# The input product of a hybrid block in fp32r high and low parts, with a reordered modulation and a reordered front

## The chip, the cores and the metric

The kernel runs on 1 core of one Trainium2 chip. The metric is the device time of one execution in microseconds. It is written by hand for the five engines (TensorE, VectorE, ScalarE, GpSimd and the DMA queue of SyncE); each engine runs its own list of instructions in order, and semaphores tie them together.

## The reference, cut to what matters

The sequence has 512 tokens (T), the model 1024 columns (D). One layer is computed:

```python
cond = silu(c)
mod = cond @ w_ada + b_ada                      # 6 x 1024: shift1, scale1, gate1, shift2, scale2, gate2
n1 = rms_norm(h, g_norm1) * (1 + scale1) + shift1
z  = n1 @ w_in                                  # 1024 -> 3840: conv GLU input | q | k | v | gate logits
branch_a = conformer_conv(z[:, :1024])          # GLU, depthwise conv over 31 taps, layer norm, swish, 512 -> 1024
attn = window_attention(q, k, v, sinks)         # 8 heads, own chunk and the one before
branch_b = attn @ w_attn_out
merged = sigmoid(gA) * branch_a + sigmoid(gB) * branch_b
h = h + gate1 * (merged @ w_out)
n2 = rms_norm(h, g_norm2) * (1 + scale2) + shift2
h = h + gate2 * peer(n2)                        # product-key retrieval over 16384 experts
out = rms_norm(h, g_final)
```

The change touches everything up to `n2`. The PEER part behind it is the same in both kernels.

## The kernel before

All activations lie transposed, columns of the model on the 128 partitions and the 512 tokens along them: `hT` and `nT` are 8 such tiles (KT = 8) of 128x512. A tile of the input product is 128 output columns by 512 tokens: 8 matmuls that accumulate over k into one PSUM bank. The product has 30 such tiles: 8 for the convolution (a GLU half and its gate in turn), 4 for q, 1 for k, 1 for v (which is computed the other way round, tokens on the partitions, in 4 x 8 matmuls of 128x128), and 16 for the gates.

**Modulation.** `w_ada` comes as 48 chunks of 128x1024 (0.5 MB), 8 for each of the six rows of `mod`, through a ring of four in `low` (`load_ada`, L293). VectorE multiplies each chunk by one column of `cond` and adds it up in `macc` (L1032, L1035). TensorE then sums `macc` over the partitions with 8 matmuls against a single column of ones (`modulation`, L495). The first 16 chunks are needed for `n1`; the others are taken in between the convolution's GLU products, and their sums over the partitions stand inside the attention, in `att_scores` at a = 3, 5, 7 and 9.

**Head.** SyncE issues four chunks, then `xT`, then the other twelve. ScalarE squares `hT`, TensorE sums the squares (`column_sums`, L488), VectorE makes the reciprocal of the root, scales `hT` into `nT`, and ScalarE applies scale and shift (`modulate`, L788).

**Input product.** `product` (L503) is a plain fp32 matmul; in the profile one fp32 matmul appears as two MATMUL records. Weights come as pairs of tiles (1 MB) through the ring of four pairs `wring`; the q, k and v weights have a place of their own (`qkvw`, 3 MB in one load). Convolution tiles and q, k, v run through four PSUM banks in turn (`bank`, `bank_free`).

**Attention.** 16 steps `att_out(a)`, a = 4 b + m for four token blocks b and four pairs of heads m. TensorE's order within a step is: transposes of the probabilities (L570, waits for `p_ready`), scores of step a+2 (L548), gate tile a+1 (L503), output product (L582, waits for `pt_ready`). VectorE adds the bias, takes the maximum, and divides by the sum (`att_norm`, L1078), and works off the convolution's taps in between: 124 taps (31 for each of four tiles) of one `scalar_tensor_tensor` over 128x512 (L1092), 44 of them ahead of the attention. ScalarE takes the exponentials (L832), copies the transposed probabilities out (L818), once per block the output (L821, waits for `o_done`), and the gate tiles (L825).

**Behind it.** Sum for the layer norm, attention projection and convolution projection (fp32, L503), merged with the gates by VectorE; then the output product `w_out`, which already works in two parts: ScalarE rounds a weight tile to fp32r (`wout_round`, L855), VectorE takes the remainder (`wout_rest`, L1155), and TensorE forms high x high, high x low and low x high in 24 matmuls for a tile (L640). Then the second norm and the PEER part: query product, selection of keys on VectorE and GpSimd, and dense expert products in fp32r (L702, L744) to the end.

Of the kernel before, what the change touches and what calls it, by code (L numbers as in the profile page):

```python
# [7 lines left out]
P = 128  # L8
D = 1024
T = 512  # L10
KT = D // P
TB = T // P
CT = 4
TAPS = 31
TAPS_BEFORE = 11
# [32 lines left out]
R_CONV, R_GATE, R_PROJ, R_WOUT, R_PQ, ROUNDS = 0, 1, 3, 4, 5, 7  # L48
MODS = 6

# [11 lines left out]
N_WOUT = N_PROJ + 2 * KT - 4  # L62
# [6 lines left out]
def build(nc, stream, wada, wqkv, skT, xT, cols, rows, biasd, identd, puT, pu, pv, gmat, hsave, out):  # L69
# [4 lines left out]
    with ExitStack() as ctx:  # L74
# [10 lines left out]
        place.close()  # L85
        big = sb("big", [P, 22 * D])
# [5 lines left out]
        qkvw = mid[:, :].rearrange("p (j k c) -> p j k c", j=6, k=KT)  # L92
# [18 lines left out]
        wparts = place.enter_context(nc.sbuf_tensor("wparts", [P, 2, 2, D], f32r))  # L111
        place.close()
        ptsb = sb("ptsb", [P, 2, 4, P])
# [39 lines left out]
        macc = gates[:, 2 * KT - 2 * MODS:2 * KT, :].rearrange("p (q a) t -> p q (a t)", q=MODS)  # L153
# [58 lines left out]
        MOD2 = ps[:, 3, KEYS:KEYS + MODS * KT]  # L212

# [3 lines left out]
        qkvw_here = sem("qkvw_here")  # L217
# [5 lines left out]
        ada_used, macc_ready = sem("ada_used"), sem("macc_ready")  # L223
# [55 lines left out]
        def _(sp):  # L279
            sp.dma_start(colv[:, :], cols).then_inc(small_here, 16)  # L280

            def load_round(r, wait):
                for s in range(4):
                    if wait:
                        sp.wait_ge(pair_begun, r * 4 + s - 2)
                    sp.dma_start(wring[:, s, :, :, :].rearrange("p a b c -> p (a b c)"),
                                 stream[bass.ds(r * 4 + s, 1), :, :].rearrange("a p f -> (a p) f")
                                 ).then_inc(w_here[s], 16)
            def load_ada(g, wait):
                for e in range(4):  # L290
                    if wait:
                        sp.wait_ge(ada_used, g * 4 + e - 3)
                    sp.dma_start(aring[:, e, :], wada[bass.ds(g * 4 + e, 1), :, :].rearrange("a p f -> (a p) f")  # L293
                                 ).then_inc(ada_here[e], 16)
            load_ada(0, False)
            sp.dma_start(hT, xT).then_inc(x_here, 16)
            with sp.Fori(1, 2 * KT // 4) as g:
                load_ada(g, True)
            load_round(0, False)
            sp.dma_start(mid[:, :], wqkv).then_inc(qkvw_here, 16)  # L300
            with sp.Fori(2 * KT // 4, MODS * KT // 4) as g:
                load_ada(g, True)
            sp.dma_start(ident[:, :], identd).then_inc(late_here, 16)
            sp.dma_start(rowv[:, :], rows).then_inc(late_here, 16)
            sp.wait_ge(ada_used, MODS * KT)
            sp.dma_start(bias, biasd).then_inc(late_here, 16)
            sp.dma_start(skw, skT).then_inc(late_here, 16)
            with sp.Fori(1, ROUNDS) as r:
                load_round(r, True)
# [7 lines left out]
            sp.wait_ge(pair_begun, 4 * (ROUNDS - 1) + 2)  # L317
# [60 lines left out]
        def _(pool):  # L378
            nc.gpsimd.memset(ones[:, :], 1.0).then_inc(consts, 1)
            nc.gpsimd.memset(eps[:, :], EPS).then_inc(consts, 1)  # L380
# [10 lines left out]
            nc.gpsimd.memset(zeros[:, :], 0.0).then_inc(consts, 1)  # L391

# [84 lines left out]
        def _(pe):  # L477
# [5 lines left out]

            def column_sums(n, sq0, count):
                o = bank(n)
                for k in range(count):
                    pe.wait_ge(sq_ready, sq0 + k + 1)
                    mm = nc.tensor.matmul(o, ones[:, :], sq[:, (sq0 + k) % 2, :], start=(k == 0), stop=(k == count - 1))  # L488
                    mm.then_inc(sq_used if k < count - 1 else tile_done, 1)

            def modulation(q):

                pe.wait_ge(macc_ready, q + 1)
                for c in range(KT):
                    mm = nc.tensor.matmul((MOD if q < 2 else MOD2)[:, q * KT + c:q * KT + c + 1], macc[:, q, c * P:(c + 1) * P], ones[:, 0:1],  # L495
                                          start=True, stop=True)
                return mm
# [16 lines left out]
            for s in range(4):  # L514
                pe.wait_ge(w_here[s], (R_CONV + 1) * 16)
                for j in range(2):
                    mm = product(bank(N_CONV + 2 * s + j), lambda k: wring[:, s, j, k, :], lambda k: nT[:, k, :], begins=j == 0,
                                 need=0 if s == 0 and j == 0 else None)
                    mm.then_inc(tile_done, 1)


            pe.wait_ge(qkvw_here, 16)
            for j in range(5):
                mm = product(bank(N_QKV + j), lambda k: qkvw[:, j, k, :], lambda k: nT[:, k, :])
                mm.then_inc(tile_done, 1)
            o = bank(N_QKV + 5)
# [976 lines left out]
```

## Time and profile before

| | us |
|---|---|
| median of 3 runs | 1781.67 |
| lowest, highest | 1777.55, 1782.49 |
| the profiled execution's own time | 1778.79 |
| its span | 1776.4 |

The profiled execution's time is 2.4 us more than its span, and lies 2.9 us below the median. The page gives, for each engine, busy time and its share of the span. A stage's busy time says which engine leads there, and the chain of waits says what TensorE waited for. A granted clock of 1.00 stands for 2.4 GHz and one of 0.50 for 1.2 GHz.

| stage | from, to (us) | what runs |
|---|---|---|
| head | 0, 41.9 | first norm, modulation rows 0 and 1 |
| convolution tiles and q, k, v | 41.9, 141.1 | 14 tiles of the input product |
| attention | 141.1, 289.3 | 16 steps, 16 gate tiles |
| projections, output product | 289.3, 395.4 | |
| second norm, PEER | 395.4, 1776.4 | same in both kernels |

### The profile page before, as it was taken

What the parts mean: (1) busy time and instruction counts of PE and PEld (TensorE: products, weight loads), DVE (VectorE), ACT (ScalarE), POOL (GpSimd) and SP (SyncE); (2) the same over time, 40 slices, a digit from 0 to 9 for tenths busy, and PEclk for the clock granted to TensorE, in tenths of its full rate; (3) what the DMA queues carried; (4) which work ended last, traced back from release to release, by engine and by line L of the source; (5) the groups of instructions that cost most, each with busy time, mean ns of one, the idle gap of its engine ahead of it and who ended that gap; (6) DMA issues with size and microseconds to landing.
All of it is one profiled execution on the core that took longest, in us unless ns stands there. A gap on an engine that the chain in (4) does not pass through costs nothing. (4 is left out here: it accounts for less than half of the span.)

```text
span 1776.4 us, 23708 instructions
## 1 busy us (share of the span) xinstructions
PE 1679.0 (95%) x7829; PEld 1331.5 (75%) x7829; DVE 1352.0 (76%) x2820; ACT 543.3 (31%) x751; POOL 442.4 (25%) x386
## 2 busy tenths in 40 slices
PE   3999999998998799898999999999999999999995
PEld 2445544474446799897898998989889989898984
DVE  6677664534999799995878787878787877878787
ACT  2102233223112356663322223232222222323222
POOL 0000000001456500001333333333343343334330
PEclk8999999999998999999999999999999999999998
DMA  9951110321212235457897878888888888788872
GB/s 358 337 218 48 57 62 24 112 79 53 90 36 72 72 137 211 164 202 289 301 320 277 325 275 312 288 296 302 294 296 298 310 288 307 282 320 325 325 289 96
DMA packets 137982, 388.46 MB, mean 219 GB/s; under 512 B 9408, under 2 KB 58816, under 8 KB 132160
## 3 DMA queue, kind: packets, MB, share of 16 engines
q1 hardware_dynamic: 99904, 251.33, 39.7%
q0 software_dynamic: 36864, 134.23, 20.4%
q10 hardware_dynamic: 1152, 2.10, 0.3%
q8 instruction: 35, 0.57, 0.1%
q14 instruction: 27, 0.22, 0.0%
HBM read 358.26 MB, written 29.36 MB: 218 GB/s over the span
## 5 line engine op out<-in xcount | busy, mean ns | idle before, releaser
L702 PE MATMUL ps<-xs,Us 128*128 128x384 f32 x3072 | 566.4, 340 | 12.6 <-POOL Us L427 10.2
L702 PEld LDWEIGHTS ps<-xs,Us 128*128 128x128 f32 x3072 | 544.4, 190 | 23.2 <-POOL Us L427 12.1
L744 PE MATMUL ps<-Vs,As 128*128 128x512 f32 x2304 | 544.0, 392 | 5.9 <-DVE Vs L1373 5.9
L744 PEld LDWEIGHTS ps<-Vs,As 128*128 128x128 f32 x2304 | 432.5, 188 | 93.4 <-DVE Vs L1373 5.8
L503 PE MATMUL ps<-big 128*128 128x512 f32 (+1 forms) x784 | 327.7, 577 | 9.8 <-ACT big L788 9.8
L503 PEld LDWEIGHTS ps<-big 128*128 128x128 f32 x784 | 144.3, 193 | 179.4 <-issue 175.3
L975 ACT ACTIVATE att<-ps 128x384 f32<-128x384 f32 x96 | 47.2, 492 | 594.2 <-PE ps L702 594.2
L463 POOL DMA_INDIRECT big<-pv,islot x128 | 156.5, 1223 | 211.1 <-DVE low L1390 174.0
L463 POOL DMA_INDIRECT big<-pu,islot x128 | 144.3, 1128 | 218.0 <-DVE dot L1378 182.9
L1364 DVE TENSOR_TENSOR att<-att 128x384 f32<-128x384 f32 x96 | 53.4, 557 | 161.5 <-ACT att L975 151.6
L1390 DVE SCALAR_TENSOR_TENSOR low<-big,act_w,low 128x1024 f32<-128x1024 f32 x128 | 158.5, 1280 | 1.2 <-DMA big<-pv,islot 1.2
L1373 DVE TENSOR_TENSOR Vs<-big,Vs 128x1024 fp32r<-128x1024 f32 x128 | 156.0, 1219 | 3.1 <-ACT Vs L978 3.1
L978 ACT ACTIVATE Vs<-big 128x1024 fp32r<-128x1024 f32 x128 | 134.9, 1054 | 68.6 <-PE ps L744 56.7
L1378 DVE CUSTOM_DVE_ANT_0 big<-big,ptsb 128x1024 f32<-128x1024 f32 x128 | 151.4, 1221 | 0.0
L890 ACT ACTIVATE Us<-big 128x1024 fp32r<-128x1024 f32 x128 | 134.3, 1049 | 36.4 <-DMA big<-puT 35.1
L454 POOL COPY islot<-eidx 128x8 int32 (+1 forms) x32 | 31.8, 993 | 367.7 <-DMA gmat<-big 208.2
L1350 DVE TENSOR_TENSOR Us<-big,Us 128x1024 fp32r<-128x1024 f32 x95 | 116.0, 1221 | 4.3 <-ACT Us L890 2.1
L388 POOL TENSOR_TENSOR xs<-big,xs 128x384 fp32r<-128x384 f32 x8 | 7.8, 1009 | 412.9 <-ACT xs L874 412.9
L729 PE MATMUL ps<-low 128*128 128x128 f32 x768 | 93.2, 280 | 15.1 <-ACT big L948 8.6
L1339 DVE TENSOR_SCALAR low<-iotan,att 128x128 f32<-128x128 f32 x384 | 106.9, 344 | 0.0
L729 PEld LDWEIGHTS ps<-low 128*128 128x128 f32 x768 | 91.7, 196 | 16.3 <-DVE low L1339 10.0
L948 ACT ACTIVATE big<-ps 128x512 f32<-128x512 f32 x96 | 93.6, 1140 | 5.6 <-PE ps L729 5.6
(163 smaller groups left out, 1296.2 us busy)
## 6 DMA issues: line engine op xcount, KB each, us to landing
big<-puT SPq DMA_DIRECT2D x128, 512.0 KB, 4.9
big<-pv SPq DMA_DIRECT2D x64, 1024.0 KB, 8.9
big<-stream SPq DMA_DIRECT2D x28, 1024.0 KB, 4.8
low<-wada SPq DMA_DIRECT2D x48, 512.0 KB, 5.2
gmat<-big SPq DMA_DIRECT2D x12, 2048.0 KB, 7.3
att<-gmat SPq DMA_DIRECT2D x32, 768.0 KB, 9.5
big<-wqkv SPq DMA_DIRECT2D x1, 3072.0 KB, 19.9
big<-xT SPq DMA_DIRECT2D x1, 2048.0 KB, 11.2
```

Of the source, the lines that this page charges most:

```text
L463: nc.gpsimd.indirect_dma_start(out=row[:, r % ROWBUF, :], out_offset=None, in_=table, in_offset=bass.IndirectOffsetOnAxis(ap=islot[:, half ...
L503: mm = nc.tensor.matmul(o, lhs(k), rhs(k), start=(k == 0), stop=(k == count - 1))
L702: mm = nc.tensor.matmul(ps[:, 6 + e, 0:DT], a, xs[:, b, k, :], start=(k == 0 and a is hi and b == 0), stop=(k == KT - 1 and a is lo))
L729: mm = nc.tensor.matmul(ps[:, c, t * P:(t + 1) * P], ohj[:, 4 * c + t, :], ohi[:, 4 * c + t, :], start=True, stop=True)
L744: mm = nc.tensor.matmul(ps[:, 2 * b + half, :], a, Vs[:, e, w, half * T:(half + 1) * T], start=False, stop=(last and a is lo))
L890: f(Us[:, e, 0, :], uraw[:, e, :], ACT.Copy).then_inc(uhi_ready, 1)
L978: f(Vs[:, d % 2, 0, :], vraw[:, d // 2 % 2, d % 2, :], ACT.Copy).then_inc(vhi_ready, 1)
L1339: mm = v.tensor_scalar(ohi[:, 4 * c + t, :], iotan[:, :], lists[:, 0, tok:tok + 1], lists[:, 2, tok:tok + 1], ALU.is_equal, ALU.mult)
L1350: v.tensor_tensor(Us[:, e, 1, :], uraw[:, e, :], Us[:, e, 0, :].bitcast(f32), ALU.subtract).then_inc(ulo_ready, 1)
L1373: v.tensor_tensor(Vs[:, a, 1, :], vraw[:, d // 2 % 2, d % 2, :], Vs[:, a, 0, :].bitcast(f32), ALU.subtract).then_inc(vlo_ready, 1)
L1378: v.tensor_tensor_reduce(out=row[:, s % ROWBUF, :], in0=row[:, s % ROWBUF, :], in1=n_tok, scale=1.0, scalar=0.0, op0=ALU.mult, op1=ALU.add ...
L1390: v.scalar_tensor_tensor(acc[:, s % 2, :], row[:, s % ROWBUF, :], act_w[:, bass.ds(g * DOTS + (s - SLOTS), 1)], acc[:, s % 2, :], ALU.mult ...
```

## The change

**Input product in parts.** Each tile of it is now formed as `w_out` is: ScalarE rounds the weight tile to fp32r (`w_round`, into a ring of HIS = 3 high parts `whi`), another engine subtracts the rounded from the full weight (`wlo`), and TensorE runs `three`: high weight x high n1, high x low, low x high, 24 fp32r matmuls for a tile in place of 8 fp32 ones. The v tile does the same with 96 matmuls of 128x128. `n1` is split too: ScalarE writes the rounded `ahi` (`n1_round`), VectorE the full value (`n1_fp32`) and the remainder `alo` (`n1_rest`). The first two tiles advance together over k. VectorE makes the weight remainders of tiles 0 to 16 (`w_rest`); GpSimd makes those of the last 13 gate tiles, during the attention.

**Modulation.** Chunks 0 to 15 are no longer added up by VectorE: TensorE takes each in 8 fp32 matmuls with a single column of `cond` as the moving operand (`eat`), one chunk behind each of the 8 sums of squares and then 8 more. Chunks 16 to 23 go through VectorE among the convolution tiles, chunks 24 to 47 through VectorE behind the attention (their loads wait for the scores of the last step); row 2 is summed over the partitions at a = 3 of the attention, rows 3 to 5 between the output product and the second norm's sums.

**Loads.** `xT` now goes ahead of all chunks. The q, k, v weights come through the ring of pairs, as tiles 8 to 13.

**Attention.** Two gate tiles run ahead (AHEAD = 2), the division by the sum moves to ScalarE (`att_scale`, two instructions, behind the gate tile's copy and the rounding), the sink's exponential is two instructions, taps are spread as 5 in a step, 47 of them ahead of the attention.

**Projections.** All 8 attention projections run ahead of the 8 convolution projections, with the layer norm's sums in between.

```diff
-            pe.wait_ge(consts, 1)
-            column_sums(N_RMS1, 0, KT)
-            modulation(0)
-            modulation(1).then_inc(mod_done, 1)
+            def eat(i):
+                q, k = divmod(i, KT)
+                pe.wait_ge(ada_here[i % 4], 16 * (i // 4 + 1))
+                for c in range(KT):
+                    mm = nc.tensor.matmul(MOD[:, q * KT + c:q * KT + c + 1], ada_slot(i)[:, c * P:(c + 1) * P],
+                                          cond[:, k:k + 1], start=False,
+                                          stop=(i == 2 * KT - 1 and c == KT - 1))
+                mm.then_inc(ada_eaten, 1)
...
+            def three(o, j, k, begins=False):
+                hi, lo = whi[j % HIS][:, k * P:(k + 1) * P], wlo[:, j // 2 % 4, j % 2, k, :]
+                for w, a in ((hi, ahi), (hi, alo), (lo, ahi)):
+                    mm = nc.tensor.matmul(o, w, a[:, k, :], start=(k == 0 and w is hi and a is ahi),
+                                          stop=(k == KT - 1 and w is lo))
...
+            o = bank(N_RMS1)
+            for k in range(KT):
+                column_sum(o, 0, k, KT)
+                eat(k)
+            for k in range(KT):
+                eat(KT + k)
+            pe.wait_ge(wlo_ready, 2)
+            pair = [bank(N_CONV), bank(N_CONV + 1)]
+            for k in range(KT):
+                pe.wait_ge(n1lo_ready, k + 1)
+                for j in range(2):
+                    mm = three(pair[j], j, k, begins=(j == 0 and k == 0))
...
-                if a + 1 < TB * PAIRS:
-                    gate_tile(a + 1)
+                if a + AHEAD < TB * PAIRS:
+                    gate_tile(a + AHEAD)
...
+            pe.wait_ge(attn_merged, KT)
+            for q in range(3, MODS):
+                mm = modulation(q)
+            mm.then_inc(mod_done, 1)
             column_sums(N_RMS2, KT + CT, KT)
...
+            def w_round(j):
+                p = j // 2
+                act.wait_ge(w_here[p % 4], w_count(p))
+                if HIS <= j < 2 * P_GATE + HIS:
+                    act.wait_ge(tile_done, N_CONV + j - HIS + 1)
+                elif j >= HIS:
+                    act.wait_ge(gate_done, j - HIS - 2 * P_GATE + 1)
+                f(whi[j % HIS], wring[:, p % 4, j % 2, :, :].rearrange("p k c -> p (k c)"), ACT.Copy).then_inc(whi_ready, 1)
...
                 if a >= 1:
                     att_evac(a - 1)
-                    gate_evac(a - 1)
+                gate_evac(a)
+                if 2 * P_GATE + a + HIS < FRONT:
+                    w_round(2 * P_GATE + a + HIS)
+                att_scale(a)
...
+            for j in range(2 * P_GATE + HIS, FRONT):
+                pool.wait_ge(whi_ready, j + 1)
+                pool.wait_ge(wlo_ready, j)
+                nc.gpsimd.tensor_tensor(wlo[:, j // 2 % 4, j % 2, :, :].rearrange("p k c -> p (k c)"),
+                                        wring[:, j // 2 % 4, j % 2, :, :].rearrange("p k c -> p (k c)"),
+                                        whi[j % HIS].bitcast(f32), ALU.subtract).then_inc(wlo_ready, 1)
```

## Rows read from the trace of the kernel before

**Rows 1.** Page: the span, and TensorE's busy time, share and instructions.
```profile
span 1776.4 us, 23708 instructions
PE 1679.0 (95%) x7829; PEld 1331.5 (75%) x7829; DVE 1352.0 (76%) x2820; ACT 543.3 (31%) x751; POOL 442.4 (25%) x386
```

**Rows 2.** Busy time by stage: PE, PEld, DVE, ACT, POOL, clock, DMA share, GB/s.
```profile
0.00:41.90 41.90, 14.13 (x48) 8.48 (x49) 26.55 (x25) 9.32 (x14) 0.81 (x8) 0.84 0.92 353
41.90:141.10 99.20, 98.28 (x272) 47.40 (x273) 70.90 (x84) 12.31 (x19) 0.00 (x0) 0.98 0.70 260
141.10:289.30 148.20, 147.49 (x552) 71.78 (x552) 91.82 (x211) 36.07 (x115) 0.00 (x0) 0.99 0.16 57
289.30:395.40 106.10, 106.10 (x339) 63.40 (x338) 44.49 (x57) 32.59 (x36) 0.00 (x0) 1.00 0.22 80
```

**Rows 3.** DMA rate over the first 20 us, one value per 0.5 us.
```profile
GB/s 0 0 0 37 275 262 377 369 393 410 262 254 295 393 377 492 475 557 328 360 459 492 459 360 426 344 385 352 442 426 418 410 410 434 426 401 270 279 311 295
```

**Rows 4.** ScalarE in order of time: start, us, line, tiles, idle before.
```profile
14.34 1.15 ACT L778 ACTIVATE att<-big 128x512 f32<-128x512 f32 x2 [11.37 <-DMA big<-xT]
226.09 0.60 ACT L821 ACTIVATE attnT<-ps 128x512 f32<-128x512 f32 x1 [9.39 <-PE ps L582]
```

**Rows 5.** TensorE in order of time, the same columns.
```profile
23.83 1.84 PE L495 MATMUL ps<-ones,gates 128*128 128x1 f32 x16
34.60 3.58 PE L495 MATMUL ps<-ones,gates 128*128 128x1 f32 x16 [8.93 <-DVE gates L1035]
177.93 8.83 PE L503 MATMUL ps<-big 128*128 128x512 f32 x16
227.23 7.13 PE L503 MATMUL ps<-big 128*128 128x512 f32 x16
236.11 7.13 PE L503 MATMUL ps<-big 128*128 128x512 f32 x16
351.00 44.52 PE L640 MATMUL ps<-mparts,wparts 128*128 128x512 f32 x192
```

**Rows 6.** Short stretches with TensorE's granted clock, columns as in rows 2.
```profile
34.60:38.20 3.60, 3.58 (x16) 3.49 (x16) 3.40 (x2) 0.00 (x0) 0.00 (x0) 0.50 1.02 430
42.00:45.00 3.00, 3.00 (x4) 1.41 (x5) 1.34 (x3) 3.00 (x5) 0.00 (x0) 0.50 1.05 451
...
175.00:178.00 3.00, 3.00 (x27) 2.48 (x27) 0.00 (x0) 0.38 (x1) 0.00 (x0) 1.00 0.03 5
178.50:181.50 3.00, 3.00 (x5) 1.35 (x4) 2.83 (x10) 0.00 (x0) 0.00 (x0) 0.50 0.28 49
195.50:198.50 3.00, 3.00 (x30) 2.81 (x32) 0.00 (x0) 1.08 (x2) 0.00 (x0) 1.00 0.00 0
```

**Rows 7.** Matmul groups by shape: count, busy us, mean ns of one, idle before.
```profile
L702 PE MATMUL ps<-xs,Us 128*128 128x384 f32 x3072 | 566.4, 340 | 12.6 <-POOL Us L427 10.2 <-issue 2.1 <-DVE Us L1350 0.3
L503 PE MATMUL ps<-big 128*128 128x128 f32 x64 | 7.3, 275 | 0.0
```

**Rows 8.** Groups by shape on ScalarE, VectorE and GpSimd, columns as in rows 7.
```profile
L855 ACT ACTIVATE wparts<-big 128x1024 fp32r<-128x1024 f32 x8 | 8.4, 1057 | 31.5 <-PE ps L640 25.0 <-DMA big<-stream 6.4
L788 ACT ACTIVATE big<-big,mod,coef 128x512 f32<-128x512 f32 x16 | 11.5, 802 | 19.2 <-DVE coef L1047 14.9 <-DVE big L1017 4.3
...
L1373 DVE TENSOR_TENSOR Vs<-big,Vs 128x1024 fp32r<-128x1024 f32 x128 | 156.0, 1219 | 3.1 <-ACT Vs L978 3.1
L1092 DVE SCALAR_TENSOR_TENSOR work<-work,colv 128x512 f32<-128x512 f32 x120 | 80.9, 746 | 0.0
...
L427 POOL TENSOR_TENSOR Us<-big,Us 128x1024 fp32r<-128x1024 f32 x11 | 28.0, 2553 | 10.4 <-ACT Us L890 10.1 <-POOL attnT L412 0.3
```

**Rows 9.** One VectorE group twice, and GpSimd beside the second, by time.
```profile
442.30 0.69 DVE L1258 TENSOR_TENSOR big<-att 128x64 f32<-128x64 f32 x5
...
588.49 2.49 DVE L1258 TENSOR_TENSOR big<-att 128x64 f32<-128x64 f32 x5
...
586.98 2.37 POOL L407 TENSOR_TENSOR low<-low,att 128x1024 f32<-128x1024 f32 x1
```

More of the change, by code:

```diff
@@ L308, in _ @@
-            with sp.Fori(1, ROUNDS) as r:
-                load_round(r, True)
+            for p in range(4, P_WOUT):
+                load_pair(p)
+            sp.wait_ge(s_done, TB * PAIRS)
+            for i in range(3 * KT, 4 * KT + 4):
+                load_ada(i)
+            load_pair(P_WOUT)
+            for i in range(4 * KT + 4, 5 * KT):
+                load_ada(i)
+            load_pair(P_WOUT + 1)
+            for i in range(5 * KT, 5 * KT + 4):
+                load_ada(i)
+            load_pair(P_WOUT + 2)
@@ L311, in load_u @@
+            load_pair(P_WOUT + 3)
+            for i in range(5 * KT + 4, CHUNKS):
+                load_ada(i)
+            sp.wait_ge(ada_used, CHUNKS - 2 * KT)
+            sp.dma_start(skw, skT).then_inc(skw_here, 16)
+            for p in range(P_PQ, STREAM):
+                load_pair(p)
             def load_u(n, e):
@@ L522, in _ @@
[L522 to L524 removed]
+            def three(o, j, k, begins=False):
[3 more added lines that the diff above has]
+                                          stop=(k == KT - 1 and w is lo))
+                    if begins and w is hi and a is ahi:
+                        mm.then_inc(pair_begun, 1)
+                return mm
@@ L525, in _ @@
                 mm.then_inc(tile_done, 1)
-            o = bank(N_QKV + 5)
+            j = 2 * P_GATE - 1
+            o = bank(N_CONV + j)
+            pe.wait_ge(wlo_ready, j + 1)
             for b in range(TB):
-                mm = product(o[:, b * P:(b + 1) * P], lambda k: nT[:, k, b * P:(b + 1) * P], lambda k: qkvw[:, 5, k, :])
+                for k in range(KT):
+                    hi, lo = whi[j % HIS][:, k * P:(k + 1) * P], wlo[:, j // 2 % 4, j % 2, k, :]
+                    for a, w in ((ahi, hi), (alo, hi), (ahi, lo)):
+                        mm = nc.tensor.matmul(o[:, b * P:(b + 1) * P], a[:, k, b * P:(b + 1) * P], w,
+                                              start=(k == 0 and a is ahi and w is hi), stop=(k == KT - 1 and w is lo))
@@ L589, in _ @@
             att_scores(1)
-            gate_tile(0)
+            for g in range(AHEAD):
+                gate_tile(g)
             for a in range(TB * PAIRS):
@@ L1059, in _, with glu @@
+            def glu(m):
                 n = N_CONV + 2 * m
@@ L1145, in _ @@
                 v.tensor_tensor(y[:, m, :], y[:, m, :], rstd, ALU.mult).then_inc(yn_ready, 1)
+            chunk(3 * KT + 1)
+            for d in range(3, KT):
+                attn_merge(d)
+                chunk(3 * KT + d - 1)
+            chunk(4 * KT - 1)
             def merged_rest(d):
```

475 lines of the change are left out of this document (282 added, 193 removed).

## Prediction

> **What bounds the kernel now.** The page comes first: TensorE is busy for 95% of the span [rows 1], so time is won only where its own work gets shorter or a wait of its goes away. The split by stage says where: in the convolution, q, k, v stage, in the attention and in the projections TensorE is busy for 98.3 of 99.2, 147.5 of 148.2 and 106.1 of 106.1 us, while VectorE has 71 to 92 us of the first two and ScalarE 12 to 36 [rows 2]. There TensorE's matmul time is the stage's length, and the other engines have room. The head is another matter: TensorE is busy for 14 of 41.9 us, and the DMA queue moves 353 GB/s at 92% busy [rows 2]; the first 16 modulation chunks and x are 10.5 MB, and they set its end. The last thing to read is TensorE's clock: the head ran at 0.84 on average, and the short stretches show which work it did before the clock rose or fell [rows 6].
>
> **The tile in parts.** The 14 tiles took 98.28 us; less 7.3 for the v tile [rows 7] and 1.6 for the start at 1.2 GHz (half of the 3.1 us from 41.9 to 45.0) [rows 6], 13 fp32 tiles took 89.4, or 6.88 each. The output product has the new form already: 192 matmuls for 8 tiles in 44.52 us [rows 5], or 5.57 a tile, with rounding and remainders hidden. So a tile saves 1.31 us. The v tile goes from 64 records in 7.3 us to 96 matmuls of 128 columns, which no row shows in fp32r. Lower bound: at the old rate of a record, (7.3 / 64) x 96 = 11.0. Upper bound: at the pace of the 384-column fp32r matmuls, 566.4 / 3072 = 0.184 each, 17.7; at a whole fp32 matmul each (0.228) 21.9. It would be 5.9 at best, if time went by columns alone (0.184 / 3). I take 11.0, since weight loads are as many and as wide as in the old record. **Convolution, q, k, v: -13 x 1.31 + 3.7 = -13.3.**
>
> The side work there is hidden: for a tile a rounding of 1.05 us on ScalarE and a remainder of 1.22 on VectorE [rows 8] beside 5.57 of matmuls. VectorE also has up to 5 taps of 0.67 (80.9 / 120), together 4.6 us, and a GLU product in every second tile. A chunk of modulation takes about the time of a remainder, and 16 chunks have left VectorE. Were this cover gone, each tile would wait some tenths.
>
> **The head.** Now TensorE does 16 chunks of 8 single-column matmuls. The same form is in the trace twice: 8 of them took 1.84 us at full clock and 3.58 at half clock [rows 5, 6]. Adding up the rates of the first 20 us [rows 3], x and the small columns (2.2 MB) are there at 8.2 us, where ScalarE waited for x until 14.3 before [rows 4]; the first sum starts at 9.0. A sum of squares is 0.86 (an eighth of 6.88), 1.72 at 1.2 GHz. A chunk comes each 1.5 us (0.5 MB at 353 GB/s) and is then no longer what is waited for: TensorE needs 1.84 or 3.58.
> Which clock? At 34.6 TensorE ran single-column matmuls for 3.58 us without a pause and the clock stayed at 0.50 to their end and beyond; full-width matmuls from 41.9 on brought it to 2.4 GHz after 45 (the convolution stage as a whole has 0.98) [rows 2, 6]. At 175 it was never idle, did transposes, the single-column matmuls and scores for 3 us, and the clock fell to 0.50 all the same; the full-width tile behind took 8.83 instead of 7.13 [rows 5, 6]. The same mixture at 195.5 kept 1.00 [rows 6]. I read: single-column matmuls do not lift the clock, and may lose it. In the new head they take two thirds of TensorE's time up to the eighth sum, and all of it behind that. I take 1.2 GHz throughout: 9.0 + 8 x (1.72 + 3.58) + 8 x 3.58 = 80.0. Then coefficients 0.4, two `n1_round` of 0.72 (11.5 / 16), two roundings of 1.05, a remainder of 1.22 [rows 8]: the first product starts at 85.2, against 41.9. **Head: +43.3.** At full clock it would be 9.0 + 8 x 2.70 + 8 x 1.84 + 1.7 (start at half clock) = 47.0, and 52.2 with the rest: +10.3. This is the term that decides.
> By the Trainium skill (TensorE: Matmul & The Clock Gate, the section on the HAM clock gate) the halved clock is the default and activity releases it; single-column matmuls aren't set apart. By that alone the head would come out at the +10.3; the row at 34.6 speaks against it here.
>
> **Attention.** A step lasts 8.88 us, from gate tile to gate tile [rows 5]. 16 gate tiles save 16 x 1.31 = 21.0. Three of four modulation sums leave (3 x 1.84 = 5.5), and the tile of 8.83 loses 1.7. Against that stands a new wait. `att_scale` is on ScalarE's queue. At a = 4, 8 and 12 ScalarE waits for the block's last output product, as it did before at 226.09 [rows 4], but now behind that wait are queued the output's copy (0.6), a gate copy (0.6), `w_round` (1.05) and the two scalings (0.4 each, estimated as half of 0.72 for half the width), and TensorE's next transposes wait for the last. TensorE has nothing to do meanwhile, since the gate tile stands behind the transposes: 3.0 each, 9.0. The second last step has no gate tile any more to cover ScalarE: 1.0. The pauses follow on small matmuls, so I add the price of a half-clock stretch, 1.7, at 0.7 of three places: 3.6. Between the ends of 0 and 5.1. **-21.0 - 5.5 - 1.7 + 9.0 + 1.0 + 3.6 = -14.6.**
>
> GpSimd's 13 remainders take 2.55 us each [rows 8], and were idle time there; one is wanted each 7 us or more, two steps ahead. They can slow VectorE: five small adds took 0.69 alone and 2.49 while a GpSimd operation of 2.37 ran [rows 9]. At worst 13 x 2.55 = 33 us come on top of VectorE's 92, 125 in all against some 133 of stage: hidden as a sum, and I take 0. The Trainium skill (SBUF — State Buffer, Who interferes with whom) says a VectorE instruction with two SBUF inputs contends with a GpSimd one that reads SBUF, and whoever comes second is fully blocked; the trace agrees [rows 9]. Every tap is of that kind, so this speaks against giving the remainders to GpSimd, where VectorE itself would need 1.22.
>
> **Behind it.** fp32 projections are the same in number, 106.1 us with TensorE never idle [rows 2]. The first now waits for ScalarE's last copy: 0.9. VectorE has a chunk more per tile, and two remainders at d = 5, so the last `merged_rest` comes about 1.5 late. Three modulation sums come between output product and second norm, where nothing covers them: 5.5. They are single-column again, so part of them and of the sums of squares behind runs at 1.2 GHz: 3.0 (from 0 to 5.5). **+10.9.** The q, k, v weights in the ring, later loads (SyncE now waits for the last scores before chunk 24) and `skT` come when DMA is at 16 to 22% [rows 2]: 0. PEER is unchanged: 0.
>
> **Sum.** +43.3 - 13.3 - 14.6 + 10.9 = +26.3. On the profiled execution's 1778.8 that gives 1805.1. That execution lies 2.9 below the median, well inside the range.
>
> **Rivals.**
> 1. Head at full clock (the page's rule): 33.0 less, -6.7, 1772.1: faster. For it: 195.5 kept its clock, and each sum of squares is a full-width matmul. Against it: 34.6 and 175 [rows 6]. It decides from the clock being above half for nearly all of the 16 chunks; break-even is a head of about 59 us. 0.10.
> 2. The first eight chunks, mixed with sums, at full clock, the last eight at half: 9.0 + 21.6 + 1.7 + 28.6 = 60.9, 19.1 less, +7.2: 1786.0, about no change. 0.14.
> 3. Half clock, and in addition GpSimd's lock makes VectorE late in each step (13 x 0.5 = 7), or the v tile costs its upper 17.7 to 21.9 (7 to 11 more): 1812 to 1823. 0.10.
> 4. The parts do not pay in the front (weights come late, a tile still takes 6.88): 29 x 1.31 = 38 more, 1843. The output product's rows speak against it. 0.02.
> My forecast has 0.64.
>
> **How the numbers follow.** The forecast's own range is 1789 (v tile 5.9, no half-clock patches, shorter waits) to 1816. About 0.3% is what a measurement of this kernel can tell from no change. Faster: rival 1 and a little error of the sum in rival 2, 0.14. Same: most of rival 2, 0.11. Slower: the forecast, rivals 3 and 4 and a rest of 2, 0.75. The range 1781 to 1821 leaves out rival 1 and the ends.
>
> **What would show it.** The granted clock and the length of the single-column matmuls between 9 and 80 us: pieces of 3.58, then the first full-width tile at 85; pieces of 1.84 and a start at 52 would refute me. Tiles of 5.5 us between; v tile near 11; three idle times of 3 us of TensorE released by ScalarE's scaling; three modulation sums ahead of the second norm. If the product starts at 85 and the time is still below 1790, my prices behind it are wrong.

## The result

The changed kernel takes 1814.62 us (median of 4 runs, 1813.72 to 1817.79) against 1782.08 us (4 runs, 1777.55 to 1783.28) for the kernel before on the same chip: ratio 1.019, 95% interval 1.017 to 1.021. It is slower, by 32.5 us. The forecast was 1805.1 us in a range from 1781 to 1821.

The profiled execution of after took 1817.79 us, with a span of 1816.0 (3 above its median, as that of before lies 3 below its own, so the spans differ by 39.6). Busy time by stage, columns as in [rows 2]; the boundaries are the first product, the first scores of the attention, the wait ahead of the first attention projection, and the second norm's sums of squares:

```profile
0.00:84.60 84.60, 69.00 (x274) 60.57 (x274) 13.21 (x18) 14.01 (x20) 0.95 (x9) 1.00 0.55 199
84.60:169.30 84.70, 83.81 (x409) 70.76 (x409) 65.46 (x86) 23.28 (x29) 0.00 (x0) 1.00 0.33 120
169.30:306.70 137.40, 126.63 (x632) 94.39 (x632) 98.43 (x159) 65.81 (x178) 31.05 (x13) 0.94 0.17 62
306.70:432.10 125.40, 118.28 (x386) 72.14 (x385) 72.88 (x82) 33.49 (x36) 0.00 (x0) 0.95 0.49 176
432.10:1816.00 1383.90, 1317.51 (x6622) 1143.52 (x6622) 1115.86 (x2446) 453.26 (x569) 438.30 (x377) 0.98 0.67 239
```

Set beside the stages of before, this gives the account that the forecast can be held against:

| stage | before | after | difference | forecast |
|---|---|---|---|---|
| head | 41.9 | 84.6 | +42.7 | +43.3 |
| convolution, q, k, v | 99.2 | 84.7 | -14.5 | -13.3 |
| attention | 148.2 | 137.4 | -10.8 | -14.6 |
| projections, output product, modulation sums | 106.1 | 125.4 | +19.3 | +10.9, with the sums of squares |
| second norm, PEER | 1381.0 | 1383.9 | +2.9 | 0 |

Of the last +2.9, the sums of squares account for 2.2: they take 9.83 where they took 7.59.

**The head.** TensorE in order of time, columns as in [rows 5]. A chunk of eight single-column matmuls takes 3.41 us, a sum of squares 2.05, and the last nine chunks 30.72 together (144 records, 16 a chunk, 3.41 each); then TensorE waits 6.07 us for VectorE's remainder:

```profile
10.11 2.07 PE L541 MATMUL ps<-att,ones 128*128 128x512 f32 x2 [6.43 <-ACT att L876]
11.97 3.41 PE L554 MATMUL ps<-cond,low 128*128 128x1 f32 x16
...
47.81 30.72 PE L554 MATMUL ps<-cond,low 128*128 128x1 f32 x144
84.61 0.80 PE L580 MATMUL ps<-ahi,whi 128*128 128x512 f32 x1 [6.07 <-DVE wlo L1187]
...
88.19 0.61 PE L580 MATMUL ps<-ahi,wlo 128*128 128x512 f32 x1
88.61 0.42 PE L580 MATMUL ps<-ahi,whi 128*128 128x512 f32 x1
```

The 3.41 is the half-clock length, as at 34.6 us of before (3.58), and not the 1.84 of full clock [rows 5]. The page's clock, however, says 1.00 for this stretch. The pace contradicts it: the product's own matmuls begin each 0.43 us until 88.6 and each 0.23 from then on, as at a clock that doubles there. So the column can't be read in this head, and whether it is the clock needs an experiment of its own (below).

**Attention and behind it.** First the attention's group of transposes with its idle time (columns as in [rows 7]), and one of the three places where most of it arises, in order of time, which is ScalarE's `att_scale`, as forecast. Then TensorE from the first output product:

```profile
L660 PE MATMUL ps<-ident,att 128*128 128x128 f32 x56 | 10.5, 309 | 9.4 <-ACT att L954 9.4
```

```profile
215.00 1.12 PE L660 MATMUL ps<-ident,att 128*128 128x128 f32 x4 [2.92 <-ACT att L954]
...
373.58 3.71 PE L731 MATMUL ps<-mparts,wparts 128*128 128x512 f32 x15 [2.30 <-DVE wparts L1335]
377.91 0.97 PE L731 MATMUL ps<-mparts,wparts 128*128 128x512 f32 x3 [0.62 <-DVE mparts L1330]
381.10 0.97 PE L731 MATMUL ps<-mparts,wparts 128*128 128x512 f32 x3 [2.23 <-DVE mparts L1330]
383.14 42.82 PE L731 MATMUL ps<-mparts,wparts 128*128 128x512 f32 x171 [1.06 <-DVE mparts L1330]
425.80 6.43 PE L563 MATMUL ps<-ones,work 128*128 128x1 f32 x48
432.09 9.83 PE L541 MATMUL ps<-att,ones 128*128 128x512 f32 x16
447.90 12.64 PE L571 MATMUL ps<-big 128*128 128x512 f32 x22 [5.99 <-ACT big L886]
```

The output product ran without a pause in 44.52 us before [rows 5]; here it waits four times, 6.2 us in all (2.3 of them ahead of it), and lasts 52.2, from 373.6 to 425.8. The forecast had 1.5 for that. ScalarE in order of time shows who is late:

```profile
356.36 2.00 ACT L994 ACTIVATE wparts<-big 128x1024 fp32r<-128x1024 f32 x2 [16.79 <-DMA big<-stream]
358.27 1.13 ACT L1000 ACTIVATE mparts<-gates 128x512 fp32r<-128x512 f32 x2
```

ScalarE rounds the first two tiles of `w_out` (L994) ahead of all merged tiles (L1000). It stands 16.8 us for their load. Not all of that holds something up: VectorE's first merged tile (L1348) is there at 348.84, so merged tiles wait behind the load for 7.5 us, up to 356.36. SyncE issues the load at 351.57:

```profile
345.76 1.77 SPq L319 DMA_DIRECT2D low<-wada  x2
351.57 0.33 SPq L311 DMA_DIRECT2D big<-stream  x1
```

Two things make it late. Its place in the ring is that of the pair which the convolution projections read, and these now come behind all attention projections; that wait is 4.0 us, from 347.53 on. And twelve chunk loads, most of which wait for VectorE, stand ahead of it in SyncE's queue until 347.53, so without the ring it would still have come only 4.0 us earlier. The load itself takes the last 4.8 us. The forecast put these loads at 0, since the DMA engines had room; what was late was not the bandwidth but the place in the ring and in SyncE's queue.

### The profile page after: what moved, and what is told of

Same layout as the page of the kernel before. It is cut to its first block and busy times, and to the rows that moved or that the text cites. A ratio compares the mean times of both kernels' runs of the same rounds, so it can differ in the third digit from the quotient of the medians.

```text
span 1816.0 us, 24572 instructions
## 1 busy us (share of the span) xinstructions
PE 1715.2 (94%) x8319; PEld 1441.4 (79%) x8319; DVE 1365.8 (75%) x2790; ACT 589.8 (32%) x830; POOL 470.3 (26%) x399
## 5 line engine op out<-in xcount | busy, mean ns | idle before, releaser
L800 PE MATMUL ps<-xs,Us 128*128 128x384 f32 x3072 | 568.5, 340 | 14.4 <-POOL Us L482 10.1
L518 POOL DMA_INDIRECT big<-pv,islot x128 | 151.8, 1186 | 211.8 <-DVE low L1570 174.0
L509 POOL COPY islot<-eidx 128x8 int32 (+1 forms) x32 | 36.0, 1124 | 362.3 <-DMA gmat<-big 205.9
L571 PE MATMUL ps<-big 128*128 128x512 f32 x256 | 114.2, 605 | 6.0 <-ACT big L886 6.0
L827 PEld LDWEIGHTS ps<-low 128*128 128x128 f32 x768 | 91.7, 196 | 14.6 <-DVE low L1519 9.0
L580 PE MATMUL ps<-ahi,whi 128*128 128x512 f32 x232 | 95.9, 413 | 6.1 <-DVE wlo L1187 6.1
L571 PEld LDWEIGHTS ps<-big 128*128 128x128 f32 x256 | 49.1, 194 | 66.1 <-issue 64.5
L439 POOL TENSOR_TENSOR wlo<-big,whi 128x1024 fp32r<-128x1024 f32 x13 | 31.0, 2388 | 254.5 <-ACT whi L903 254.5
```

The lines of the kernel that those rows point to most:

```text
L518: nc.gpsimd.indirect_dma_start(out=row[:, r % ROWBUF, :], out_offset=None, in_=table, in_offset=bass.IndirectOffsetOnAxis(ap=islot[:, half ...
L571: mm = nc.tensor.matmul(o, lhs(k), rhs(k), start=(k == 0), stop=(k == count - 1))
L800: mm = nc.tensor.matmul(ps[:, 6 + e, 0:DT], a, xs[:, b, k, :], start=(k == 0 and a is hi and b == 0), stop=(k == KT - 1 and a is lo))
L827: mm = nc.tensor.matmul(ps[:, c, t * P:(t + 1) * P], ohj[:, 4 * c + t, :], ohi[:, 4 * c + t, :], start=True, stop=True)
```

## The experiments

The first reading to be tested is the sum's own: the head costs 33 us more than at full clock; the parts pay; the rest is given back at three waits or uncovered pieces (the `att_scale` queue, the `w_out` load, the modulation sums). The rivals are a head bound by something other than the clock, parts that don't pay, and GpSimd's lock on VectorE. All edits are to the changed kernel. "before" is 1781.3, 1781.4 or 1782.9 us in the three groups of runs, each of which ran on another chip. The changed kernel itself wasn't run again in them, so a difference to it is one between groups. From the medians the four edits that win something give 32.6, 9.8, 7.6 and 5.2 us; from the ratios to before they give 33.5, 9.4, 6.8 and 7.8. The two agree within 3 us, and no single gain is known better than that.

**The head undone.** Chunks 0 to 15 go through VectorE again, and TensorE sums the two rows (L601 there).

```diff
-            for k in range(KT):
-                column_sum(o, 0, k, KT)
-                eat(k)
-            for k in range(KT):
-                eat(KT + k)
+            column_sums(N_RMS1, 0, KT)
+            for q in range(2):
+                pe.wait_ge(ada_eaten, (q + 1) * KT)
+                for c in range(KT):
+                    mm = nc.tensor.matmul(MOD[:, q * KT + c:q * KT + c + 1], macc[q][:, c * P:(c + 1) * P], ...)
```

> The changed kernel with its head alone undone: the first 16 chunks go through VectorE again and TensorE sums them over the partitions with 16 single-column matmuls; x still goes ahead, everything behind the head is as changed. My theory (the head is what loses): the first product starts at about 46 us instead of 84.6, that is the 41.9 of before plus 4 for rounding and remainders, and the time falls by 38 to 40 us, to about 1776. Rival (the loss lies in what follows, and the head only hid it, so that VectorE or the loads are late by as much once the head is short): less than 25 us come back, over 1790.

Measured: 1782.05 us (1779.97 to 1784.59, 10 runs), ratio to before 1.0003 (0.9994 to 1.0013), 32.6 us below the changed kernel. The first product starts at 49.46:

```profile
35.37 3.57 PE L601 MATMUL ps<-ones,gates 128*128 128x1 f32 x16 [9.91 <-DVE gates L1237]
49.46 0.80 PE L583 MATMUL ps<-ahi,whi 128*128 128x512 f32 x1 [10.52 <-DVE wlo L1190]
```

TensorE idles again here, and that is cheap: up to the last chunk, at 35.3 us, their DMA sets the pace (342 GB/s over the whole head). So the head decides the sign: with it undone, the rest of the change comes out at nothing, 1782 against 1781. It starts 3.5 later than I expected, because VectorE takes the reciprocal and the scaling of `hT` (35.2 to 43.4) only behind the last chunk. Of the 35.15 us by which the product starts earlier, 33.9 arrive in the span (1816.0 to 1782.1).

**Does TensorE lose the clock, or did it never have it?** 24 fp32 matmuls of 128 columns ahead of the first sum, while TensorE waits anyway.

```diff
+            for _ in range(24):
+                nc.tensor.matmul(ps[:, 5, 0:P], zeros[:, :], ones[:, :], start=True, stop=True)
```

> The changed kernel with 24 extra fp32 matmuls of 128 columns on TensorE ahead of the first sum of squares, where it waits for x anyway, so that the clock is up when the chunks begin. My theory (single-column matmuls don't hold the clock): the first one or two chunks take 1.84 us each, then the pace is 3.4 again, and the first product starts at 80 to 83 us. Rival (the head is slow only because it never had an unbroken start; a clock that is up stays up under this work): chunks at 1.84 throughout, product at about 50 us, time near 1780.

Measured: one run, 1813.33 us; the product starts at 81.93. TensorE in order of time, then two stretches as in [rows 2]:

```profile
11.65 1.02 PE L541 MATMUL ps<-att,ones 128*128 128x512 f32 x2
12.51 1.84 PE L554 MATMUL ps<-cond,low 128*128 128x1 f32 x16
14.21 1.10 PE L541 MATMUL ps<-att,ones 128*128 128x512 f32 x2
15.16 2.67 PE L554 MATMUL ps<-cond,low 128*128 128x1 f32 x16
...
19.54 3.41 PE L554 MATMUL ps<-cond,low 128*128 128x1 f32 x16
```

```profile
0.00:16.00 16.00, 12.85 (x79) 11.93 (x79) 0.00 (x0) 3.90 (x6) 0.95 (x9) 1.00 0.73 274
16.00:49.00 33.00, 33.00 (x120) 26.80 (x121) 1.48 (x1) 4.49 (x6) 0.00 (x0) 0.50 0.33 109
```

The first chunk ran at 1.84; in the second the clock fell, and from 16 us the column reads 0.50 while TensorE is busy without a pause. After that every length is that of the changed kernel's head, 2.05 and 3.41. So these lengths are those of 1.2 GHz, and the mixture of chunks and sums of squares itself loses the clock. This refutes the forecast's rival 1, full clock all through, and its rival 2, full clock in the mixed half.

**Is it the clock, or the pace of weight loads?** After each four single-column matmuls one more full-width matmul over `hT`, whose result isn't used.

```diff
+                    if c % 4 == 3:
+                        pe.wait_ge(x_here, 16)
+                        nc.tensor.matmul(ps[:, 5, :], ones[:, :], hT[:, 0, :], start=True, stop=True)
```

> The changed kernel with one full-width fp32 matmul into a spare bank behind every 4 single-column ones of the head (two for each chunk, 32 in all). At full clock a chunk is then 1.84 + 1.72 = 3.6 us, at half clock 3.4 + 3.4 = 6.8. My theory (what TensorE does in its columns decides the clock): the added work brings the clock up within the head, single-column groups of 4 fall from 1.7 to 0.92 us, and the head ends at 75 to 95 us although TensorE does more. Rival (3.4 us for a chunk is the pace of weight loads or of issue and no matter of the clock): groups of 4 stay at 1.7 us, and the product starts at 84.6 + 32 x 0.86 = 112 or later.

Measured: one run, 1822.05 us; the product starts at 87.04, 2.4 later than in the changed kernel, with 32 more full-width matmuls in the head. TensorE across the point where the pace changes:

```profile
23.39 1.71 PE L554 MATMUL ps<-cond,low 128*128 128x1 f32 x8
24.96 2.05 PE L561 MATMUL ps<-big,ones 128*128 128x512 f32 x2
26.81 1.78 PE L541 MATMUL ps<-att,ones 128*128 128x512 f32 x2
28.43 0.95 PE L554 MATMUL ps<-cond,low 128*128 128x1 f32 x8
29.24 1.10 PE L561 MATMUL ps<-big,ones 128*128 128x512 f32 x2
```

Near 28 us all lengths halve, those of the single-column matmuls too (1.71 to 0.95 for four). The instructions are the same on both sides, so neither issue nor weight loads explain the 3.41; the clock does. The added work eats what the clock gives, and the kernel gains nothing.

**Are the parts worth anything?** The input product back in plain fp32 (and no rounding, no remainders), with the head and the orders of the changed kernel. ScalarE's queue is shorter by the roundings, and GpSimd's remainders are gone too.

```diff
-                for w, a in ((hi, ahi), (hi, alo), (lo, ahi)):
-                    mm = nc.tensor.matmul(o, w, a[:, k, :], ...)
+                mm = nc.tensor.matmul(o, wring[:, j // 2 % 4, j % 2, k, :], nT[:, k, :], ...)
```

> The changed kernel with the input product alone in plain fp32 again: no rounding and no remainders of the weights, none of n1, the rest (head, order, moved scaling, loads) as changed. Theory (a tile in parts saves 1.31 to 1.37 us, the v tile costs 3.4, and ScalarE's rounding is 1.05 of each 3 us pause): convolution, q, k, v 98 us instead of 84, attention about 21 minus 3 us longer, so 1814.6 + 14 + 18 = about 1847, with the product starting 3 us earlier, 1844. Rival (the parts win nothing in the attention since something else than TensorE sets its steps there): attention as long as now, 1825.

Measured: one run, 1844.40 us. The two stages, convolution with q, k, v and the attention, columns as in [rows 2]:

```profile
80.82:180.43 99.61, 98.73 (x272) 47.53 (x273) 47.19 (x67) 11.61 (x18) 0.00 (x0) 1.00 0.32 114
180.43:329.40 148.97, 141.03 (x504) 65.75 (x504) 77.38 (x158) 52.99 (x164) 0.00 (x0) 1.00 0.16 57
```

By the spans (1842.4 and 1816.0) the parts are worth 26.4 us, so the forecast's rival 4 is refuted: 14.9 in the first stage, 11.6 in the attention, less 3.8 that the product starts later for the roundings and remainders, and 3.7 in the stages behind, whose code is the same. The attention should give 16 x 1.42 = 22.7 (below). It gives half of that: in fp32 it idles 7.9 us with the clock at 1.00, in parts 10.8 us with the clock at 0.94, which is 8.2 us lost in 137.4. The lengths bear out the 1.00: each fp32 gate tile there took 7.13 us or less. Without the rounding in ScalarE's queue the three waits are 1.98 to 1.99 us instead of 2.9. The time of 1844 was met in part by luck: the attention was expected to be about 18 us longer and was 11.6, and 3.7 came from stages that weren't edited.

**The `att_scale` queue.** The two scalings go ahead of the gate copy and the rounding.

```diff
                     att_evac(a - 1)
+                att_scale(a)
                 gate_evac(a)
                 if 2 * P_GATE + a + HIS < FRONT:
                     w_round(2 * P_GATE + a + HIS)
-                att_scale(a)
```

> The changed kernel with one move in ScalarE's order of an attention step: the two scalings stand ahead of the gate tile's copy and of the weight rounding. Theory (TensorE's three idle times of 2.9 us are ScalarE's queue behind the block's last output product): copy and rounding, 1.5 us, leave each of them, which go to 1.4 us; with less half-clock matmuls behind them 4 to 8 us are won in all, 1807 to 1811. Rival (the pause is VectorE's lateness with the sums, and ScalarE only shows it): the idle times stay at 2.9 us and the time at 1814.

Measured: 1804.78 us (1804.72 to 1805.20, 4 runs), ratio to before 1.0138 (1.0109 to 1.0167): 9.8 less, more than expected. The idle time in front of the transposes halves, and the first projection starts at 300.0 instead of 307.6. The group (columns as in [rows 7]) and the stretch (as in [rows 2]):

```profile
L660 PE MATMUL ps<-ident,att 128*128 128x128 f32 x56 | 9.6, 287 | 4.6 <-ACT att L954 4.5
```

```profile
169.30:300.00 130.70, 123.84 (x632) 92.57 (x632) 101.97 (x159) 67.06 (x180) 33.87 (x13) 0.96 0.19 65
```

The waits give 4.8 us. Much of the rest comes with the clock, 0.96 against 0.94 in the attention and 0.98 against 0.96 in the 119 us behind it (from 300.0, and from 306.7 of the changed kernel), where nothing was edited; and the output product waits 4.9 us instead of 6.2. One profile can't show that such a phase of the clock repeats; what four runs hold is the 9.8 us as a whole.

**GpSimd's lock on VectorE.** VectorE makes the last 13 remainders itself.

```diff
-            for j in range(2 * P_GATE + HIS, FRONT):
-                ... nc.gpsimd.tensor_tensor(wlo[...], wring[...], whi[...], ALU.subtract) ...
+                if 2 * P_GATE + a + HIS < FRONT:
+                    w_rest(2 * P_GATE + a + HIS)
```

> The changed kernel with the weight remainders of the last 13 gate tiles made by VectorE, behind each step's sums, and none by GpSimd. Theory (VectorE has the room, and GpSimd's work costs TensorE nothing): attention within 1 us of now, the time the same, 1814, and VectorE's taps get shorter, 0.67 each throughout. Rival (GpSimd locks VectorE out so long that steps are late): 5 to 7 us faster, 1808. Other rival (VectorE in its turn waits for ScalarE's rounding and is late for the next scores): some us slower.

Measured: 1813.53 us (1810.70 to 1816.67, 4 runs), ratio to before 1.0182 (1.0152 to 1.0212): no difference from the changed kernel. VectorE's groups over the attention, first of after, then of this kernel:

```profile
L1215 DVE SCALAR_TENSOR_TENSOR work<-work,colv 128x512 f32<-128x512 f32 x77 | 63.1, 883 | 0.0
L1286 DVE SCALAR_TENSOR_TENSOR nmx<-mx,nsink 128x2 f32<-128x2 f32 x16 | 11.3, 709 | 0.6
```

```profile
L1207 DVE SCALAR_TENSOR_TENSOR work<-work,colv 128x512 f32<-128x512 f32 x80 | 54.4, 745 | 0.0
...
L1278 DVE SCALAR_TENSOR_TENSOR nmx<-mx,nsink 128x2 f32<-128x2 f32 x16 | 2.6, 161 | 0.6
```

GpSimd's help is real and worth nothing. The 13 remainders (31.0 us on GpSimd, 2388 ns each) make the taps slower by 63.1 - 77 x 54.4 / 80 = 10.7 us, and a tiny operation on two columns takes 709 ns on average instead of 161, 8.7 us in all: 19.4 us lent to VectorE's queue to spare it 13 x 1.22 = 15.9. Both stay hidden, because VectorE is busy for 98 of 137 us there. The average of 709 hides two kinds: eleven of the sixteen took 0.16 us, as in this kernel, and the other five began while a remainder ran and ended within 0.02 us of its end. The first of them, with GpSimd's remainder beside it (changed kernel, by time):

```profile
183.45 2.33 DVE L1286 SCALAR_TENSOR_TENSOR nmx<-mx,nsink 128x2 f32<-128x2 f32 x1
183.37 2.39 POOL L439 TENSOR_TENSOR wlo<-big,whi 128x1024 fp32r<-128x1024 f32 x1 [3.55 <-ACT whi L903]
```

The Trainium skill (SBUF — State Buffer, Who interferes with whom) says that a VectorE instruction with two SBUF inputs contends with a GpSimd one that reads SBUF, and calls the port pair that they share an exclusive lock. The trace agrees by these rows, though this kernel's time doesn't show it.

**The `w_out` rounding later.** ScalarE rounds the first two tiles of `w_out` behind the third merged tile.

```diff
-            wout_round(0)
-            wout_round(1)
             for k in range(KT):
+                if k == 3:
+                    wout_round(0)
+                    wout_round(1)
```

> The changed kernel with ScalarE rounding the first two tiles of w_out behind the third merged tile and not ahead of the first. Theory (the ring slot of w_out's first pair comes free only in the third convolution projection; ScalarE waits 16.8 us for that load with the merged tiles queued behind it, and VectorE's merging starts 7 us late): the waits of TensorE at the beginning of the output product, 2.3 + 0.6 + 2.2 + 1.1 us, and the half-clock stretch behind them mostly go, 5 to 9 us, 1806 to 1810. Rival (VectorE's 16 modulation chunks there are too many, and it is late by itself): less than 3 us, 1812 or more.

Measured: 1807.06 us (1805.73 to 1808.26, 4 runs), ratio to before 1.0153 (1.0124 to 1.0182): 7.6 less. Of the four waits one of 1.06 is left, and no half-clock stretch follows it: the last 171 matmuls take 39.42 instead of 42.82.

```profile
370.89 5.51 PE L731 MATMUL ps<-mparts,wparts 128*128 128x512 f32 x21
377.46 39.42 PE L731 MATMUL ps<-mparts,wparts 128*128 128x512 f32 x171 [1.06 <-DVE mparts L1331]
```

**The modulation sums later.** The three sums of rows 3 to 5 go behind the second norm's sums of squares, into the time in which TensorE waits 5.99 us for the query product's input. VectorE takes the coefficients accordingly behind the reciprocal (not shown in the diff).

```diff
+            column_sums(N_RMS2, KT + CT, KT)
             pe.wait_ge(attn_merged, KT)
             for q in range(3, MODS):
                 mm = modulation(q)
             mm.then_inc(mod_done, 1)
-            column_sums(N_RMS2, KT + CT, KT)
```

> The changed kernel with the three modulation sums moved behind the second norm's sums of squares. Theory: the three sums take 6.4 us of TensorE just ahead of the sums of squares, where nothing covers them, while TensorE then stands idle for 6 us ahead of the query product; moved there they cost nothing: 1808 to 1810 us. Rival: the coefficients then come later than VectorE's scaling needs them and the idle time grows by what was won: 1812 to 1815 us.

Measured: 1809.46 us (1808.61 to 1811.37, 4 runs), ratio to before 1.0147 (1.0131 to 1.0164): 5.2 less.

```profile
425.39 1.88 PE L541 MATMUL ps<-att,ones 128*128 128x512 f32 x4
427.48 5.79 PE L541 MATMUL ps<-att,ones 128*128 128x512 f32 x12 [0.21 <-ACT att L876]
433.11 6.55 PE L563 MATMUL ps<-ones,work 128*128 128x1 f32 x48
441.74 16.78 PE L571 MATMUL ps<-big 128*128 128x512 f32 x32 [2.08 <-ACT big L886]
```

From the output product's end to the query product it is 16.4 us instead of 22.1. The idle time is 2.08 instead of 5.99, and the sums of squares run at full clock: 7.7 instead of 9.8. The rival, coefficients that come late, costs nothing that shows.

**All of it together.** Head undone, with the reciprocal at the twelfth chunk and half of the scaling behind the first two remainders; scaling first; `w_out` rounding later. Then the same with the modulation sums later too.

> All of it: the head undone as in the first run, there with the reciprocal before the 13th chunk, with the rounding and remainders of the first two weight tiles ahead of the coefficients and half of the scaled rows behind them; scaling first in the attention; w_out's rounding later. From 1782.0 of the first run: 6 us from the head (product at 43.5 instead of 49.5), 5 from the attention and 7 from the output product if they add up: about 1764, 1.0% faster than before. Rival (they overlap, as shorter waits come back as waits of the same engine further on): 1770 to 1775.

> The kernel that undoes the head, divides the sum before the remainders and makes the output weight's parts after the merge (1760.2 us), with the three modulation sums moved too. Theory: the 5.5 to 6.4 us of the sums add to the other three gains: 1754 to 1756 us. Rival, the coefficients come late: 1759 to 1762 us.

Measured: 1760.22 us (1755.82 to 1763.05, 4 runs), ratio to before 0.9885 (0.9852 to 0.9918), and with the sums 1751.60 us (1750.70 to 1756.09, 4 runs), ratio 0.9823 (0.9806 to 0.9839). The last is 31 us faster than before, and 63 faster than the changed kernel (66 by the ratios). The sum of the single edits is 32.6 + 9.8 + 7.6 + 5.2 = 55.2, and the better order in the head gives another 3.5 (49.46 to 45.93); 58.7 of the 63. Both came out a little lower than expected (1764, and 1754 to 1756). The last kernel's second modulation sum and its first product:

```profile
37.89 3.57 PE L601 MATMUL ps<-ones,gates 128*128 128x1 f32 x16 [12.26 <-DVE gates L1242]
45.93 0.77 PE L583 MATMUL ps<-ahi,whi 128*128 128x512 f32 x1 [4.47 <-DVE alo L1189]
```

The step between the two, 8.6 us, is more than the 5.2 of the sums alone; their ratios' intervals leave room for 2 to 20 us (0.9852 less 0.9839, and 0.9918 less 0.9806, of 1782), so that isn't a contradiction. By the ratios the sums alone give 7.8, and the step is 11.

## Why the prediction was right, and where its terms were not

**The head: right, term by term.** 43.3 forecast, 42.7 measured. A chunk took 3.41 (3.58 assumed), a sum of squares 1.84 from its start to the next chunk (1.72), the first sum started at 10.1 (9.0), and from the last chunk to the product it was 84.61 - 78.53 = 6.1 (5.2). The step that carried the forecast was to read the matmul form of the new head at 34.6 and 175 us of before, and to ask what the clock did under it, not only what it cost. The experiment with the earlier matmuls shows the stronger half of that reading: the clock isn't only not granted, it is withdrawn while TensorE is busy all the time. By the Trainium skill (TensorE: Matmul & The Clock Gate, the section on the HAM clock gate) the clock is throttled by default and activity releases it. The row from 16 to 49 us of that experiment, 33.00 of 33.00 us busy at 0.50, goes against it for this kind of activity. At full clock the forecast's sum has +10.3 for this head.

**Convolution, q, k, v: right.** -14.5 against -13.3. From the first product to the v tile it is 84.61 to 157.58, less 2.0 for the half-clock start, for 13 tiles: 5.46 each, where I had 5.57, taken from an output product that has its own small losses. So a tile saves 1.42, not 1.31. The v tile takes 10.8 us (157.6 to 168.4), 11.0 forecast: its rate of a record is that of the fp32 form. The mean of a record is 273 to 275 ns in its three groups of 32, as in [rows 7].

**Attention: mechanism right, the clock's terms short.** The waits were forecast at 9.0 + 1.0; all idle time rose from 0.7 to 10.8. The tiles gave 22.7 instead of 21.0, the modulation sums 5.5. What remains of -10.8 is 22.7 + 5.5 - 10.1 - 10.8 = 7.3 us more lost to half clock than before, where I had 3.6 less 1.7 = 1.9. Two steps failed. One is "at 0.7 of three places": a half-clock stretch follows each of the three waits, and the one behind the second is twice as deep (together 6.8 us where 3.6 stood). The other is "the tile of 8.83 loses 1.7": there the clock had fallen behind a modulation sum, and the sum of row 2 stays in the attention. In this profile the clock falls behind it again (188 to 196 us, another 1.7), without any wait of TensorE's. (A fifth stretch, 304 to 312, lies at half clock only from the first projection on and is counted behind the attention.)

```profile
188.00:196.00 8.00, 8.00 (x40) 6.75 (x40) 6.81 (x14) 3.64 (x11) 2.38 (x1) 0.79 0.00 0
...
212.00:220.00 8.00, 5.08 (x20) 3.54 (x19) 3.05 (x5) 6.88 (x16) 4.07 (x2) 0.79 0.09 28
...
248.00:256.00 8.00, 6.42 (x18) 4.58 (x19) 4.48 (x7) 6.28 (x17) 4.74 (x2) 0.57 0.29 100
```

The sum itself stands at the start of the first of these stretches, still at full clock:

```profile
188.10 1.84 PE L563 MATMUL ps<-ones,gates 128*128 128x1 f32 x16
```

**Behind it: +10.9 forecast, 21.5 measured** (19.3 and 2.2 of the sums of squares). This is the term that was most mis-sized. The first projection's wait (0.91) and the modulation sums (6.4, 5.5 assumed) were right. Two steps failed. "Later loads: 0" was argued from the DMA share, but the load of the first `w_out` pair waits for its place in the ring and behind the chunks in SyncE's queue, and the first instruction behind it on ScalarE's queue holds up all merged tiles: 6.2 us of waits where 1.5 stood. And the half clock behind pauses and single-column matmuls cost 8.5 (first projection 1.5, output product 52.2 - 3.9 of waits - 44.4 = 3.9 (44.4 is before's, from its start to the sums of squares), the sums of squares 2.2, the modulation sums 0.9) where 3.0 stood. The later rounding gives back 7.6 and the later sums 5.2: together 12.8 of the 21.5.

**The total.** On the profiled executions, 1817.8 against a forecast of 1805.1, the forecast was 12.7 us low: 3.8 and 10.6 for the two misses, less 0.6 and 1.2 that the head and the tiles were better, with 0.7 in PEER and 0.6 less around the span. The median lies 3.2 lower, so 9.5 us are left there. The order of the costs was right, the head first and then the waits, and so was 0 for GpSimd's remainders.

What stays open is what decides whether the clock falls behind the sum of row 2. The code doesn't alone: of the eleven profiles of the changed kernel and its ten edits, five have 0.79 over the 8 us from this sum on, and six have 1.00. The kernel with the later `w_out` rounding, whose program is the changed kernel's up to there, is among the six. In the kernel before, the clock fell behind one of four such sums. So these 1.7 us differ from one profile to the next. Open too is how much of the 9.8 of the scaling's order is clock.

## What to carry to other kernels

Single-column matmuls in number were no cheap way to fill an idle TensorE: here 16 chunks of them ran at half clock, a clock raised ahead of them was lost under them and the sums of squares between them, and they replaced a wait for a DMA stream that was going to set the end anyway. A single sum of eight may run at full clock (1.84 us) and still be followed by a half-clock tile. When a step is made faster by parts, look at the two queues that now carry more: each instruction put ahead of the one that TensorE waits for (a copy, a rounding whose load isn't there yet) is paid for; putting the waited-for one first won 10 and 8 us. Cost a moved load by the place that it needs in its ring, by what stands ahead of it in the DMA queue, and by what is queued behind its first reader, not by the bandwidth that is free.

## What the runs showed of the hardware

- With 24 matmuls of 128 columns ahead, the clock was at full speed at 12.5 us (1.84 for a chunk) and at half from 16 us on, with TensorE busy in 33.00 of 33.00 us. With a full-width matmul for each four single-column ones every length halved near 28 us (1.71 to 0.95), and stayed so to the last chunk.
- The granted clock reads 1.00 from 0 to 84.6 us in the changed kernel, while every matmul has its half-clock length, and 1.00 for a stretch before 28 us with four single-column matmuls at 1.71. With the 24 matmuls ahead it reads 0.50 from 16 us for the same lengths. The column seems to say 1.00 until the first change that was recorded: read lengths beside it.
- In the v tile an fp32r matmul of 128 columns with a new weight starts each 0.11 us (10.8 / 96); one of 512 columns each 0.23.
- A VectorE operation over two columns that takes 0.16 us took 1.19 to 2.33 us in five cases in which it began while a remainder ran on GpSimd (2.39 us), and ended within 0.02 us of the remainder each time. The 128x512 taps took 0.88 us on average instead of 0.75, up to 2.93.
- Behind a modulation sum of eight single-column matmuls in the attention, with TensorE busy throughout, the granted clock fell in 5 of 11 profiles and stayed in 6. The changed kernel is among the 5, the one with the later rounding, whose program is the same up to there, among the 6.
